# The MLP's up projection as seven products of quarter matrices, with the hidden activations kept in DRAM between up and down projection

## What is computed

```python
xs = gated_residual(xs, sq_relu_ffn(modulate(xs, norm_ffn_pre[l], sh_ms, sc_ms), ffn_w1[l], ffn_w2[l]), norm_ffn_post[l], gt_ms)
# sq_relu_ffn(h, w1, w2) = square(max(h @ w1, 0)) @ w2;  h: 1152 x 1024, w1: 1024 x 4096, w2: 4096 x 1024, all float32
```

## Time and profile before

| | |
|---|---|
| median of three runs | 3395.82 us |
| span of the profiled execution | 3390.8 us |
| TensorE busy / weight loads busy | 3137.1 / 2755.1 us |
| VectorE / ScalarE / GpSimd busy | 1816.7 / 1133.1 / 1072.9 us |
| mean granted TensorE clock | 0.946 of 2.4 GHz |
| MLP of layer 0, up(1) to the end stage | 1078.5 to 1796.7 us |
| MLP of layer 1 begins, end stage at | 2576.8 us, 3322.8 us |

### The profile page before, as it was taken

One profiled execution on the slowest core, in us unless ns is written; L12 is line 12 of the kernel. 1 busy time (PEld: TensorE's weight loads), 2 busy tenths in 40 slices (PEclk: granted clock), 3 DMA queues, 4 the chain that ended last, 5 costly groups with the idle time before them and its releaser, 6 DMA issues.

```text
span 3390.8 us, 44396 instructions
## 1 busy us (share of the span) xinstructions
PE 3137.1 (93%) x17132; PEld 2755.1 (81%) x17132; DVE 1816.7 (54%) x2527; ACT 1133.1 (33%) x1924; POOL 1072.9 (32%) x697
## 2 busy tenths in 40 slices
PE   7999868999799999999998999768699999999998
PEld 3888646899678899989987898556578899989987
DVE  3799579555476333333336555576786333333335
ACT  2333233555453112111113476533253112112112
POOL 1466346100034333323231311154444333323231
PEclk9999989999899999999999999866699999999999
DMA  5565544100032011101104332321132011101103
GB/s 199 188 223 197 170 138 122 53 1 1 26 106 75 27 48 49 49 25 49 49 26 117 125 132 73 121 79 47 45 108 75 27 49 49 49 25 49 49 25 124
DMA packets 182342, 270.68 MB, mean 80 GB/s; under 512 B 16392, under 2 KB 105520, under 8 KB 182192
## 3 DMA queue, kind: packets, MB, share of 16 engines
q1 hardware_dynamic: 182192, 268.65, 23.7%
HBM read 221.43 MB, written 47.19 MB: 79 GB/s over the span
## 4 chain that ended last, share of the span: by engine, by line
PE 74%; DVE 12%; POOL 5%; issue 4%; ACT 2%; DMA 1%; SPq 1%; POOLq 1%; DVEq 0%; ACTq 0%
PE psum L854 23%; PE psum L881 20%; PE psum L692 6%; PE psum L1904 4%; PE psum L695 3%; DVE ada_acc L298 3%; PE psum L1075 3%; PE psum L1892 2%; PE psum L1899 2%; PE psum L2203 2%; DVE mix_x L2400 1%; PE psum L463 1%; DVE mix_v L2413 1%; PE psum L2565 1%; PE psum L1102 1%
## 5 line engine op out<-in xcount | busy, mean ns | idle before, releaser
L854 PE MATMUL psum<-AT,WF 128*128 128x384 f32 x4608 | 805.3, 334 | 0.0
L854 PEld LDWEIGHTS psum<-AT,WF 128*128 128x128 f32 x4608 | 800.1, 188 | 2.5 <-POOL WF L2360 0.3
L881 PE MATMUL psum<-WF,H 128*128 128x512 f32 x3024 | 691.1, 389 | 0.0
L881 PEld LDWEIGHTS psum<-WF,H 128*128 128x128 f32 x3024 | 567.2, 188 | 116.9
L960 DVE TENSOR_TENSOR yacc<-yacc,psum 128x512 f32 x504 | 346.5, 687 | 332.2 <-PE psum L881 332.2
L940 DVE TENSOR_TENSOR relu_t<-relu_t 128x384 f32<-128x384 f32 x192 | 163.4, 851 | 607.7 <-ACT relu_t L900 607.7
L973 POOL TENSOR_TENSOR H<-relu_t,H 128x384 fp32r<-128x384 f32 x192 | 192.2, 1029 | 496.7 <-ACT H L904 496.7
L969 POOL TENSOR_TENSOR WF<-RAW,WF 128x2048 fp32r<-128x2048 f32 x30 | 138.9, 4629 | 504.7 <-ACT WF L895 504.7
L900 ACT ACTIVATE relu_t<-psum 128x384 f32<-128x384 f32 x192 | 94.3, 491 | 594.1 <-PE psum L854 588.0
L692 PE MATMUL psum<-WT,AT 128*128 128x512 f32 (+1 forms) x1296 | 285.1, 380 | 4.2 <-ACT stage L738 4.2
L692 PEld LDWEIGHTS psum<-WT,AT 128*128 128x128 f32 x1296 | 233.8, 192 | 48.3 <-ACT stage L738 4.5
(11 more groups left out here) (364 smaller groups left out, 4219.8 us busy)
## 6 DMA issues: line engine op xcount, KB each, us to landing
RAW<-ffn_w SPq DMA_DIRECT2D x64, 1024.0 KB, 5.4
ada_raw<-ada_w SPq DMA_DIRECT2D x18, 2048.0 KB, 8.0
RAW<-w_in_even SPq DMA_DIRECT2D x5, 2048.0 KB, 8.4
RAW<-w_in_odd SPq DMA_DIRECT2D x5, 2048.0 KB, 8.0
mix_x<-x_all SPq DMA_DIRECT2D x18, 512.0 KB, 3.6
feat_even<-stage SPq DMA_DIRECT2D x36, 256.0 KB, 4.7
x<-mix_x SPq DMA_DIRECT2D x18, 512.0 KB, 2.6
col_first<-ada_w SPq DMA_DIRECT2D x4, 2048.0 KB, 14.9
```

The costliest lines, as they stand in the source:

```text
L854: mm = nc.tensor.matmul(psum[:, bank, 0:TB], w1_part[a][:, k, m * P:(m + 1) * P], AT[:, b, k, tb * TB:(tb + 1) * TB], start=(k == 0 and n ...
L881: mm = nc.tensor.matmul(psum[:, 3 + bank, :], H1[:, slot, a, m, ds(i * TB + (u // 2) * P, P)], w2_part[b][:, m, (u % 2) * 512:(u % 2 + 1) ...
```

## The change

Two groups (`PLAIN` = 2) keep the old form. The other 14 groups of a layer use one level of Winograd's form of Strassen's scheme: the token matrix is cut into quarters (k-blocks 0 to 3 or 4 to 7, tokens 0 to 575 or 576 to 1151) and the group's w1 likewise (512 rows, 128 features); seven products of quarters or of sums of quarters stand for eight. A product is 2 token blocks x 4 k-blocks x 3 passes = 24 matmuls on 288 columns, so a group has 168. The products of a group are issued in the order 6, 7, 2, 5, 1 (of the next group), 3, 4 (`STEPS`). Products 1, 6, 5 and 3 go into one pair of PSUM banks one after another, each added on top, and after each ScalarE copies the running sum out (`keep`). 7 and 4 share a pair, 2 has its own; VectorE adds what was kept.

```diff
+        def plain_store(sp, l, g, m, tb):
+            sp.wait_ge(square_ready[tb], plain_nth(l, g, m) + 1)
+            sp.dma_start(hidden[l][2 * g + m, :, tb * TB:(tb + 1) * TB], relu_t[:, tb, :]).then_inc(plain_out[tb], 16)
...
+        def fast_product(pe, l, p, g):
+            pe.wait_ge(f_low, step_nth(p, g))
...
+            elif p == 6:
+                pe.wait_ge(x_kept, x_nth(1, g))
+                pe.wait_ge(s_low, S_LOW[2])
...
+            else:
+                pe.wait_ge(yz_kept, yz_nth(1, 1, g))
+            bank = {2: Y_BANK, 7: Z_BANK, 4: Z_BANK}.get(p, x_bank(g))
+            begins = p in (1, 2, 7)
+            for b in range(2):
+                for k in range(KH):
+                    for i, (x, w) in enumerate(PASSES):
+                        mm = nc.tensor.matmul(psum[:, bank + b, 0:HB], w_slot[p][:, w, k, :], TOKENS[p][x][:, k, b * HB:(b + 1) * HB],
+                                              start=(begins and k == 0 and i == 0), stop=(k == KH - 1 and i == 2), skip_group_check=not begins)
+            mm.then_inc(f_done, 1)
```

The token sums (`S1` to `S4`, each 128 x 4 x 576) are made once a layer by VectorE at the head of `mlp_vector`, between the squares of groups 0 and 1; ScalarE rounds them. The weight sums are made for every group by VectorE (four of 128 x 512), the seven high parts by ScalarE, the seven low parts by GpSimd. ScalarE's order at the head, and its loop:

```diff
+            relu(act, l, 1, 0, 0, 0)
+            token_high(s3_hi[:, :, :], s3_s4, 3)
+            relu(act, l, 1, 0, 1, 1)
+            for s in range(2):
+                act.wait_ge(x_gone[s], 16 * (5, 4)[s] * (2 * l + 1))
+            weight_high(act, l, 1, PLAIN)
+            token_high(s2_hi[:, :, :], s2_sum, 2)
+            relu(act, l, 1, 0, 2, 2)
+            weight_high(act, l, 6, PLAIN)
+            for tb in range(2):
+                relu(act, l, 1, 1, tb, tb)
+            token_high(s4_hi[:, :, :], s3_s4, 4)
+            act.wait_ge(s_low, S_LOW[2])
+            weight_high(act, l, 7, PLAIN)
+            weight_high(act, l, 2, PLAIN)
+            relu(act, l, 1, 1, 2, 2)
+            token_high(quarter(AT, 0, 0, 1), s1_sum, 1)
+            keep(1, PLAIN, p1_s[:, :])
+            act.wait_ge(s_low, S_LOW[1])
+            weight_high(act, l, 5, PLAIN)
+            weight_high(act, l, 1, PLAIN + 1)
+            weight_high(act, l, 3, PLAIN)
+            weight_high(act, l, 4, PLAIN)
...
+            for g in range(PLAIN, NG):
+                if g > PLAIN:
+                    act.wait_ge(yz_kept, yz_nth(0, 1, g - 1))
+                keep(6, g, u2_s[:, :])
+                for p in (6, 7, 2):
+                    weight_high(act, l, p, g + 1)
+                if g > PLAIN:
+                    act.wait_ge(yz_kept, yz_nth(1, 1, g - 1))
+                keep(5, g, u4_s[:, :])
+                weight_high(act, l, 5, g + 1)
+                if g + 1 < NG:
+                    act.wait_ge(yz_kept, yz_nth(0, 0, g))
+                    keep(1, g + 1, p1_s[:, :])
+                    weight_high(act, l, 1, g + 2)
+                else:
+                    hidden_high(act, l, 0)
+                    w2_split_high(act, l, 0)
+                hid_free(act, l, g, 1)
+                keep(3, g, hid[g % 2][1][:, 0:HT])
+                for p in (3, 4):
+                    weight_high(act, l, p, g + 1)
```

VectorE:

```diff
+            chain.mark(tt(s2, *part(0, 0), add))
+            chain.link(tt(s1, *part(0, 1), add))
+            tt(s3, s2, s1, sub).then_inc(s_ready, 1)
+            square_hidden(dve, l, 0, 0, 2)
+            chain.link(tt(s1, s1, part(1, 1)[0], add))
+            square_hidden(dve, l, 0, 1, 2)
+            tt(s1, s1, part(1, 1)[1], add).then_inc(s_ready, 1)
+            dve.wait_ge(s_ready, S_READY[1])
+            tt(s2, s1, s2, sub).then_inc(s_ready, 1)
+            square_hidden(dve, l, 1, 0, 0)
+            weight_sums(dve, l, PLAIN, 0)
+            square_hidden(dve, l, 1, 0, 1)
+            rest_of(s2_lo[:, :, :], s2, s2_hi[:].bitcast(F32), 2)
+            square_hidden(dve, l, 1, 0, 2)
+            dve.wait_ge(s3_low, 1)
+            chain.link(tt(s3, part(1, 0)[0], s2, sub))
+            weight_sums(dve, l, PLAIN, 1)
+            square_hidden(dve, l, 1, 1, 0)
+            tt(s3, s3, part(1, 0)[1], add).then_inc(s_ready, 1)
+            square_hidden(dve, l, 1, 1, 1)
+            rest_of(s4_lo[:, :, :], s3, s4_hi[:].bitcast(F32), 4)
+            square_hidden(dve, l, 1, 1, 2)
+            rest_of(quarter(AT, 1, 0, 1), s1, quarter(ATf, 0, 0, 1), 1)
+            for g in range(PLAIN, NG):
+                if g + 1 < NG:
+                    weight_sums(dve, l, g + 1, 0)
+                dve.wait_ge(f_done, step_nth(2, g))
+                dve.wait_ge(x_kept, x_nth(1, g))
+                hid_free(dve, l, g, 0)
+                add_up(g, 0, 0, Y_BANK, p1_s)
+                square_up(g, 0, 0)
+                if g + 1 < NG:
+                    weight_sums(dve, l, g + 1, 1)
+                dve.wait_ge(x_kept, x_nth(5, g))
+                hid_free(dve, l, g, 1)
+                add_up(g, 1, 1, Z_BANK, u4_s)
+                square_up(g, 1, 1)
+                square_up(g, 1, 0)
+                dve.wait_ge(f_done, step_nth(4, g))
+                add_up(g, 0, 1, Z_BANK, u2_s)
+                square_up(g, 0, 1)
+            for g in range(DOWN_GROUPS):
+                if g:
+                    dve.wait_ge(dn_kept, down_nth(l, g))
+                for u in range(18):
```

```diff
+        def down_products(pe, l, g):
+            pe.wait_ge(w2_low, NG * l + g + 1)
+            pe.wait_ge(hid_low, NG * l + g + 1)
...
+        def hidden_high(act, l, g):
+            act.wait_ge(hraw_in[g % 2], 32 * (g // 2 + 1))
+            if g == 0:
+                act.wait_ge(f_done, step_nth(7, NG - 1))
+            elif g == 1:
+                act.wait_ge(f_done, step_nth(3, NG - 1))
+                act.wait_ge(h_out[1], 64 * (FAST // 2))
+            else:
+                act.wait_ge(dn_sum, down_nth(l, g - 1))
...
+        def w2_split_high(act, l, g):
+            act.wait_ge(w2_in[g % 2], 16 * (NG // 2 * l + g // 2 + 1))
+            if g == 1:
+                act.wait_ge(yz_kept, 3 * FAST)
+                act.wait_ge(h_out[0], 64 * (FAST // 2))
+            nc.scalar.activation(WF[:, 1 - g % 2, 0, :], w_raw(g), ACT.Copy).then_inc(w2_high, 1)
...
         def mlp_gpsimd(pool, l):
...
+            pool.wait_ge(s_high, S_HIGH[3])
+            nc.gpsimd.tensor_tensor(s3_lo[:, :, :], s3_s4[:, :, :], s3_hi[:].bitcast(F32), ALU.subtract).then_inc(s3_low, 1)
+            for p, g in STEPS:
+                weight_low(pool, l, p, g)
+            for g in range(NG):
+                hidden_low(pool, l, g)
+                w2_split_low(pool, l, g)
...
+                if g + 2 < NG:
+                    raw_load(sp, l, g + 2)
+                elif g + 2 == NG:
+                    w2_load(sp, l, 0)
+                else:
+                    hidden_load(sp, l, 0)
+                    w2_load(sp, l, 1)
+                    hidden_load(sp, l, 1)
+                for n, (m, th) in enumerate(H_READY):
+                    cols = slice(th * HT, (th + 1) * HT)
+                    sp.wait_ge(h_ready, 4 * nth_fast(g) + n + 1)
+                    sp.dma_start(hidden[l][2 * g + m, :, cols], hid[g % 2][m][:, cols]).then_inc(h_out[g % 2], 16)
+            for g in range(2, NG):
+                hidden_load(sp, l, g)
+                w2_load(sp, l, g)
+                if g == NG - 5:
```

```diff
             pe.wait_ge(w2_low, NG * (l + 1) - 1)
-            for tb in range(3):
-                pe.wait_ge(h_low[tb], 2 * NG * (l + 1) - 2)
+            pe.wait_ge(hid_low, NG * (l + 1) - 1)
+            pe.wait_ge(dn_kept, DOWNS * (l + 1))
             ahead = [(0, 0), (0, 1), (1, 0)]
             for t, h in ahead:
...
             pe.wait_ge(w2_low, NG * (l + 1))
-            for tb in range(3):
-                pe.wait_ge(h_low[tb], 2 * NG * (l + 1))
+            pe.wait_ge(hid_low, NG * (l + 1))
             for t, h in ahead:
                 down(t, h, 1)
```

436 lines of the change are left out of this document (268 added, 168 removed).

## The result

The changed kernel takes **3368.5 us** (median of four runs, 3367.31 to 3369.7) against 3394.9 us for the kernel before (four runs beside it, 3393.55 to 3398.71): ratio **0.9925, 95% interval 0.9911 to 0.9939**. Forecast: 3378, range 3348 to 3402. The spans are 3390.8 and 3367.1 us, 23.7 less.

What follows compares the result with a forecast made beforehand. TensorE, busy 93% of the span, was taken as the bound. -73.9 + 2 x (14.2 + 7.1 + 3.1 + 3.4) = -18.3 us on the span 3390.8 gave 3372.5, plus 5.0 to the median: 3378 us, range 3348 to 3402.

Steps and rivals of the forecast that it cites:

- Rate: Fast groups' matmuls on TensorE: 134.0 ns each on 288 columns, 22.5 us a group, 73.9 us saved over 28 groups.
- weight loads set the pace: Rival, fast products: at 150 ns a matmul nothing is saved and the waits stay, 3451 us; chance 0.03.
- Others keep up: Inside a 22.5 us fast group: VectorE needs 8.0 us, ScalarE 7.0, GpSimd 9.1; all fit and cost nothing.
- The slack of the copy after product 5: ScalarE's copy before product 3 in a fast group: over at 13.9 us, needed at 16.1, slack 2.2 us.
- Head: Start of the MLP: VectorE becomes the bound, TensorE waits 14.2 us a layer before product 6.
- the 11 to 18 that the text gave as its sign: Timeline: a TensorE gap of 11 to 18 us before product 6 of group 2, ended by ScalarE's copy.
- the short head: Rival, start of the MLP: about 4 us of wait in place of 14.2, 3358 us; sign a gap under 8; chance 0.19.
- The lock: Start of the MLP: VectorE operations with two SBUF inputs stand still while GpSimd works, 12.5 us.
- the allowance for semaphores: Start of the MLP: 1 us allowed in VectorE's chain, whose last sum is then done at 114.4.
- From up to down: Before the first down product: waits of 6.2 + 0.9 = 7.1 us a layer for rounding and GpSimd's low parts.
- End stage: Group 15's last low part: TensorE waits 7.5 us against 4.37 before, +3.1 a layer.
- Clock: Slower clock after new waits at the MLP's start and before the first down product: 1.7 us each, +3.4 a layer.

Runs made afterwards that it cites:

- Experiment 4: The changed kernel with product 2 issued twice in every fast group, the second overwriting the first: 3458.45 us, ratio 1.019.
- experiments 5 and 6: The changed kernel with two and with five more VectorE additions before the first addition of each fast group: 3369.56 and 3422.28 us.
- Kernel 10: The changed kernel with product 1's copy first, w2 and first hidden values rounded early, third token sum's and last w2's low parts on VectorE: 3329.14 us, ratio 0.9814.
- experiments 1, 2, 3 and 7: On the changed kernel, singly: product 1's copy first, 3354.25 us; first w2 early, 3351.02; third sum's low part on VectorE, 3362.43; last w2 low part on VectorE, 3365.65.

## Why the prediction held, and where it did not

The forecast's mechanism is the one that happened: the saving by columns, and the waits before product 6, before the first down product and in the end stage. On the span it is -18.3 us against -23.7 measured, in time 3378 against 3368.5, inside the forecast's own range. That it came so near is in part luck, since misses in both directions cancel. Point by point:

- **Rate.** 134.0 ns a matmul on 288 columns was the line between the earlier trace rows; the measured 132.5 saves 2.73 x 28 = 76.4 us in place of 73.9. The line was good to 1.5 ns, 7.1 us over 28 groups. Against it, the forecast took an old group as the length of its row, 25.15 us, where the next one starts 24.99 after it; that is 4.5 us the other way. Experiment 4 gives the same price by itself.
- **Weight loads.** The rival "weight loads set the pace" fell: 4704 loads of the full array hid behind 288 columns. The Trainium skill (TensorE: Matmul & The Clock Gate, Part 3) lists loads as overlapping only across different row groups; the estimate of 227 ns from that and from the page's price of a load (its Part 2) was 132.5 here, so the measurement decides against it for this kernel.
- **Others keep up.** The slack of the copy after product 5 was forecast at 2.2 us, and experiments 5 and 6 measure 2.1; its price beyond that is 26 us for each us, not the 28 of the text, as group 15 has none of it. The squares (L1181) were longer than priced, 1.27 us on average in place of 0.75: 56 of the 112 took longer, each of these beside a GpSimd operation. They stand behind the copy's chain, and the slack held.
- **Head, the step that failed in size.** Forecast 14.2, measured 10.0 (both layers), just under the 11 to 18 that the text gave as its sign, and above the 8 of the short head. The lock itself was priced well: VectorE lost 2.1 + 2.1 + 5.0 + 1.1 + 1.1 = 11.4 us to GpSimd up to the last sum, forecast 12.5. The rest of the miss is small things in one direction: the forecast took a chain of 42.9 us (1071.5 to 1114.4), it was 39.5. 1.1 of the 3.4 is the lock; 1.0 is the allowance for semaphores, which back-to-back work did not need; 1.3 is the pace of the operations, 2.47 us from start to start where 2.6 was taken. ScalarE's tail was 6.1 in place of 6.6, and TensorE came 0.4 later, counted from the first sum. The stores of the ReLU buffers were not as free as the text had them, with 8 us to spare: the ReLU of 1084.59 stood 7.60 us idle, and its row names a store. That cost TensorE nothing visible, since VectorE's chain ran on without a gap.
- **From up to down.** 5.6 + 0.85 against 6.2 + 0.9. ScalarE and GpSimd followed one another as written, and GpSimd's second part took 5.03 us instead of 4.6, held by a square.
- **End stage.** 0.98 + 6.61 - 4.37 = 3.2 a layer against 3.1.
- **Clock, too small.** Forecast 3.4 a layer, measured 5.4 in layer 0: 2.1 behind the head (product 6 to product 2 took 8.46 us, 1118.24 to 1126.70, where 48 matmuls at 132.5 ns are 6.36), 2.2 behind the first down product, and 1.1 in the end stage, where 18 matmuls took 7.11 us against 5.97 in the earlier trace rows. In layer 1 the three are 2.7, 2.6 and -0.3, 5.0 together. The forecast took the 1.7 us of the earlier trace rows for each wait, and nothing for the end stage. The length of the wait alone does not set the cost: behind the same 6.6 us in the end stage the 18 matmuls took 7.11 us in layer 0, at a granted clock of 0.57, and 5.71 in layer 1, at 0.74. The row of layer 1:

```profile
3307.83 5.71 PE L1374 MATMUL psum<-WF,H 128*128 128x512 f32 x18 [6.62 <-POOL WF L1098]
```

The sum: -38.2 + 25.4 = -12.8 in layer 0, forecast -9.15 a layer. Of the difference of 3.6 us, the head makes 4.2 and the rate 1.25, less 2.0 of clock; the rest is small terms. The saving of 76 us was real, and two thirds of it went into waits at three joints that occur once a layer: none of them is in the loop. Kernel 10, experiments 1, 2, 3 and 7 together, takes back 39 us by the medians (3368.5 to 3329.14), 38 by the ratios; 36.5 of them lie in the two layers between the first token sum and the gate's matmuls, of the 51 lost. The arithmetic is the same; what changed is the order, and the engine of two low parts.

## What to carry to other kernels

When a loop is made cheaper by preparing operands (sums, splits), the loop itself is the easy part of the estimate; count the queues at its head and its end, where the preparation has no cover yet. There, put what TensorE waits for first on every queue, ahead of work that is merely due: copies that free a bank before roundings that are needed a product later. And for work that VectorE and GpSimd share, price the lock as well as the operation: the faster engine taking the slower one's work can shorten its own chain.
